# Gate and up projections of two feed-forward blocks by seven block products in place of eight, on one Trainium2 core

## The reference, cut to what matters

```
D_MODEL = 1024
SEQ = 512
D_FF = 2816

def _swiglu(x, w_gate, w_up, w_down):
    return (jax.nn.silu(x @ w_gate) * (x @ w_up)) @ w_down

def first_block(x, ...):
    f = _swiglu(_rmsnorm(x, ffn1_pre_g[l]), ffn1_w_gate[l], ffn1_w_up[l], ffn1_w_down[l])
    x = x + 0.5 * _rmsnorm(f, ffn1_post_g[l])
    ...
    f = _swiglu(_rmsnorm(x, ffn2_pre_g[l]), ffn2_w_gate[l], ffn2_w_up[l], ffn2_w_down[l])
    x = x + 0.5 * _rmsnorm(f, ffn2_post_g[l])
    return x
```

## Time and profile before

| | us |
|---|---|
| median of three runs (2074.23 to 2074.5) | 2074.49 |
| span of the profiled execution, first to last instruction | 2072.8 |
| PE busy in it | 2056.8 (99%) |
| DVE busy | 778.9 (38%) |
| ACT busy | 807.4 (39%) |
| POOL busy | 913.3 (44%) |

### The profile page before, as it was taken

The page is one execution under the profiler, slowest core; times in us unless marked ns, Lnnn a source line. Parts: engine busy times, 40 slices in busy tenths (PEclk is TensorE's granted clock), DMA queues, the critical chain, the costliest instruction groups (busy, mean ns, idle before and its releaser), DMA issues.

```text
span 2072.8 us, 24499 instructions
## 1 busy us (share of the span) xinstructions
PE 2056.8 (99%) x9912; PEld 1694.5 (82%) x9912; DVE 778.9 (38%) x1304; ACT 807.4 (39%) x1421; POOL 913.3 (44%) x468
## 2 busy tenths in 40 slices
PE   9999999999999999999999999999999999999998
PEld 8888888877788888888888887888888788888887
DVE  3111100777844111100356674711132676562112
ACT  4222322467754222222535543522234445352222
POOL 4444444246662444444434442544434443264442
PEclk9999999999999999999999999999999999999999
DMA  6333323221033333222322222333233222223331
GB/s 191 94 101 92 102 92 112 79 72 41 31 102 103 101 93 100 94 99 102 117 91 73 72 82 71 104 100 97 97 111 108 72 74 79 82 92 101 93 102 71
DMA packets 244256, 191.26 MB, mean 92 GB/s; under 512 B 6448, under 2 KB 208816, under 8 KB 243760
## 3 DMA queue, kind: packets, MB, share of 16 engines
q1 hardware_dynamic: 244144, 189.70, 29.7%
HBM read 187.58 MB, written 2.10 MB: 92 GB/s over the span
## 4 chain that ended last, share of the span: by engine, by line
PE 94%; DVE 3%; ACT 1%; issue 1%; SPq 0%; DMA 0%; POOL 0%; DVEq 0%; ACTq 0%
PE bank L1695 29%; PE bank L1697 28%; PE bank L1696 28%; PE bank L1689 3%; PE bank L1929 1%; PE bank L2097 1%; PE bank L1949 1%; PE bank L1956 1%; DVE xn L1158 0%; DVE x_tok L1163 0%; PE bank L2126 0%; PE bank L2128 0%; DVE m_sum L1669 0%; DVE br_lo L1570 0%; DMA w_raw<-in_ffn_w_up 0%
## 5 line engine op out<-in xcount | busy, mean ns | idle before, releaser
L629 POOL TENSOR_TENSOR w_lo<-w_raw,w_hi 128x1024 fp32r<-128x1024 f32 x324 | 783.5, 2428 | 868.6 <-ACT w_hi L723 867.8
L1695 PE MATMUL bank<-xt_hi,w_hi 128*128 128x512 f32 (+1 forms) x1504 | 579.4, 385 | 0.5
L1696 PE MATMUL bank<-xt_lo,w_hi 128*128 128x512 f32 (+1 forms) x1504 | 575.4, 383 | 0.0
L1697 PE MATMUL bank<-xt_hi,w_lo 128*128 128x512 f32 (+1 forms) x1504 | 575.4, 383 | 0.0
L723 ACT ACTIVATE w_hi<-w_raw 128x1024 fp32r<-128x1024 f32 x325 | 340.9, 1053 | 242.9 <-DMA w_raw<-in_ffn_w_down 142.6
L1695 PEld LDWEIGHTS bank<-xt_hi,w_hi 128*128 128x128 f32 x1504 | 282.7, 188 | 62.7 <-issue 6.7
L1697 PEld LDWEIGHTS bank<-xt_hi,w_lo 128*128 128x128 f32 x1504 | 282.7, 188 | 55.6
L1696 PEld LDWEIGHTS bank<-xt_lo,w_hi 128*128 128x128 f32 x1504 | 282.9, 188 | 53.6
L1264 DVE TENSOR_TENSOR h_raw<-bank,act_gate 128x512 f32<-128x512 f32 x44 | 30.4, 691 | 400.1 <-PE bank L1697 400.1
L1695 PE MATMUL bank<-w_hi,xt_hi 128*128 128x512 f32 (+1 forms) x456 | 178.2, 391 | 0.0
L1697 PE MATMUL bank<-w_hi,xt_lo 128*128 128x512 f32 (+1 forms) x456 | 174.5, 383 | 0.0
(11 more groups left out here) (305 smaller groups left out, 2853.9 us busy)
## 6 DMA issues: line engine op xcount, KB each, us to landing
w_raw<-in_w_in SPq DMA_DIRECT2D x132, 512.0 KB, 3.7
w_raw<-in_ffn_w_down SPq DMA_DIRECT2D x44, 512.0 KB, 3.5
w_raw<-in_ffn_w_gate SPq DMA_DIRECT2D x43, 512.0 KB, 3.7
w_raw<-in_ffn_w_up SPq DMA_DIRECT2D x43, 512.0 KB, 3.7
w_raw<-in_w_out SPq DMA_DIRECT2D x24, 512.0 KB, 3.5
w_raw<-in_w_branch SPq DMA_DIRECT2D x24, 512.0 KB, 3.3
w_raw<-in_w_qkv SPq DMA_DIRECT2D x16, 512.0 KB, 3.7
x_tok<-in_x SPq DMA_DIRECT2D x4, 512.0 KB, 6.9
```

Source lines behind the costliest of these rows:

```text
L629: pool.tensor_tensor(lo_slots[i], raw_slots[i], f32(hi_slots[i]), ALU.subtract).then_inc(lo_ready, 1)
L1695: pe.matmul(out_ap, ah, bh, start=first, stop=False)
L1696: pe.matmul(out_ap, ah, bl, start=False, stop=False)
L1697: return pe.matmul(out_ap, al, bh, start=False, stop=last)
```

## The change

From tile 3 on (`F0 = 3`) in both FFNs, the gate and the up slab of a tile are computed together. The weights of a tile form a 2 x 2 matrix of blocks (gate or up; first or second half of the 1024 features), the activation another (half of the features; half of the tokens). Their product takes eight block products, each of 4 x 3 matmuls of 128 x 128 weights on 256 columns. The change uses Strassen's scheme in Winograd's form with seven products and sums of blocks:

- activation sums, once per FFN on DVE (`x_sums`): the four quarters of x as `hi` plus `lo`, then s1 to s4; ACT and DVE split each into `xs_hi`, `xs_lo`;
- weight sums, per tile: t3, t2, t4 by DVE into the banks 6, 7, 4 (`w_sums`), t1 by POOL into `ws_raw1`; ACT makes `ws_hi` of the four, DVE `ws_lo` of three, POOL of t1;
- products, per tile on PE, in this order: first (gate by x) into bank 0 `b_x`; sixth (t2 by s2) into bank 1 `b_y`; the third of the tile before (up by s4) onto bank 2 `b_z`, where the fifth of that tile lies; second (gate by x) onto `b_x`; seventh (t3 by s3) onto `b_y`; fourth (t4 by x) into bank 3 `b_v`; fifth (t1 by s1) into `b_z`;
- between them ACT copies `b_x` (`u1`) before the second product lands on it, DVE forms u2 = `b_y` + u1 before the seventh lands on `b_y`, then u3 = `b_y` + u1, gate of the second token half = u3 - `b_v`, its up = `b_z` + u3 (`up_high`), up of the first half = `b_z` + u2 after the third product, and the two halves of `h_raw`.

`h_raw` now has a place for every tile, with `h_lo` over it, and the split of the hidden features moves from the tile after to the last tile and to the down product. Of an up slab only its second half is split. The core of the diff (names like `b_x`, `nth`, `product_count` are banks and counts of semaphores):

```
+F0 = 3
...
+                for f in range(F0, KF):
+                    if f > F0:
+                        pe.wait_ge(glo_done, nth(n, f - 1))
+                    else:
+                        pe.wait_ge(silu_done, F0 * n + 1)
+                    ready(s0 + 2 * f + 1)
+                    product(b_x, w_quarter(s0 + 2 * f, 0), x_quarter(0, 0)).then_inc(prod_done, 1)
+                    if f > F0:
+                        pe.wait_ge(u3_done, nth(n, f - 1))
+                    else:
+                        pe.wait_ge(silu_done, F0 * n + 2)
+                        pe.wait_ge(xsl_done, 4 * n + 2)
+                    pe.wait_ge(wsl_done, 3 * nth(n, f) - 2)
+                    product(b_y, w_sum(2), x_sum(2)).then_inc(prod_done, 1)
+                    if f > F0:
+                        third_product(f - 1)
+                    pe.wait_ge(u1_done, nth(n, f))
+                    product(b_x, w_quarter(s0 + 2 * f, 1), x_quarter(1, 0), onto=True).then_inc(w_used, 1)
+                    pe.wait_ge(u2_done, nth(n, f))
+                    pe.wait_ge(wsl_done, 3 * nth(n, f) - 1)
...
+                    product(b_y, w_sum(3), x_sum(3), onto=True).then_inc(prod_done, 1)
+                    pe.wait_ge(wsl_done, 3 * nth(n, f))
+                    if f > F0:
+                        pe.wait_ge(hhalf_done, nth(n, f - 1))
...
+                    product(b_v, w_sum(4), x_quarter(1, 1)).then_inc(prod_done, 1)
+                    pe.wait_ge(ws1l_done, nth(n, f))
+                    if f > F0:
+                        pe.wait_ge(h_done, f0 + f)
+                    product(b_z, w_sum(1), x_sum(1)).then_inc(prod_done, 1)
+                third_product(KF - 1)
...
+                x_sums()
+                hidden(0)
+                hidden(1)
+                for f in range(F0 - 1, KF):
+                    last = f == KF - 1
+                    if f == F0 - 1:
+                        x_sum_low(1)
+                        x_sum_low(2)
+                    elif f == F0:
+                        hidden(F0 - 1)
+                    else:
+                        up_high(f - 1)
+                    if not last:
+                        w_sums(f + 1)
+                    if f > F0:
+                        hidden_hi(f - 1)
+                    if f >= F0:
+                        second_sum(f)
+                    if not last:
+                        sum_low(f + 1, 2)
+                    else:
+                        hidden_low(0)
+                        hidden_low(1)
...
+                for f in (2, 3, 4, 5):
+                    hidden_low(f)
+                up_high(KF - 1)
+                hidden_hi(KF - 1)
+                hidden_of_lo(KF - 1)
...
+                    pool.tensor_tensor(ws_raw1[:, :], raw_slots[j][:, 0:512], raw_slots[i][:, 0:512], ALU.subtract)\
+                        .then_inc(ws1_made, 1)
+                    pool.wait_ge(ws1_made, nth(n, f + 1))
+                    pool.wait_ge(ws_made, 3 * nth(n, f + 1))
+                    pool.wait_ge(hi_ready, g + 1)
+                    pool.tensor_tensor(lo_slots[i], raw_slots[i], f32(hi_slots[i]), ALU.subtract).then_inc(lo_ready, 1)
```

More of the change, by code:

```diff
@@ L462, in gate_up_banks, with product_count, nth, wait_raw @@
         def gate_up_banks(f):
-            return ((0, 4), (1, 5))[f] if f < 2 else ((0, 1), (2, 3))[f % 2]
+            return ((0, 4), (1, 5), (2, 3))[f]
+        b_x, b_y, b_z, b_v = (bank[i][:, 0:256] for i in range(4))
+        b_t = {3: bank[6][:, :], 2: bank[7][:, :], 4: bank[4][:, :]}
+        N_F = KF - F0
+        PRODUCTS = {1: 1, 6: 2, 7: 3, 4: 4, 5: 5}
+        def product_count(n, f, i):
+            return 5 * (N_F * n + f - F0) + PRODUCTS[i]
+        def nth(n, f):
+            return N_F * n + f - F0 + 1
+        def wait_raw(eng, s):
+            eng.wait_ge(raw_in[slot_of[s]], 16 * (turn_of[s] + 1))
+        def quads(t):
+            return t.rearrange("p (k n) -> p k n", k=4)
         @block.sync
@@ L684, in _ @@
                     done = slabs_cast(k)
+            lows(done, S_FFN[1] + 2 * F0)
+            ffn(1)
+            done = S_FFN[1] + N_IN
             for l in range(LAYERS):
@@ L805, in hidden_high, with gate @@
                     act.wait_ge(h_done, f0 + 1 + f)
-                    act.activation(h_hi[:, f, :], h_raw[:, f % 2, :], ACT.Copy).then_inc(hhi_done, 1)
-                for f in range(KF):
+                    if f in (0, 6, 12, 14):
+                        act.wait_ge(prod_done, product_count(n, KF - 1, {0: 6, 6: 7, 12: 4, 14: 5}[f]))
+                    if f == 18:
+                        act.wait_ge(w_used, s0 + N_IN)
+                    act.activation(h_hi[f][:, :], h_raw[:, f, :], ACT.Copy).then_inc(hhi_done, 1)
+                def gate(f):
                     act.wait_ge(w_used, s0 + 2 * f + 1)
@@ L1833, in ffn, with x_quarter, x_sum, w_quarter @@
                             turn_chunk(b, 1 + q)
-                for f in range(2, KF):
+                def x_quarter(k0, c0):
+                    sl = slice(256 * c0, 256 * c0 + 256)
+                    return lambda k: (xt_hi[:, 4 * k0 + k, sl], xt_lo[:, 4 * k0 + k, sl])
+                def x_sum(m):
+                    return lambda k: (xs_hi[m][:, k, :], xs_lo[m][:, k, :])
+                def w_quarter(s, k0):
+                    return lambda k: slab(s, 4 * k0 + k, KD, P)
+                def w_sum(m):
+                    return lambda k: (ws_hi[m][:, k, :], ws_lo[m][:, k, :])
@@ new lines, in product, with third_product @@
+                def product(dst, w, x, onto=False):
+                    for k in range(4):
+                        (wh, wl), (xh, xl) = w(k), x(k)
+                        pe.matmul(dst, wh, xh, start=k == 0 and not onto, stop=False, skip_group_check=onto)
+                        pe.matmul(dst, wh, xl, start=False, stop=False, skip_group_check=onto)
+                        ins = pe.matmul(dst, wl, xh, start=False, stop=k == 3, skip_group_check=onto)
+                    return ins
+                def third_product(f):
+                    pe.wait_ge(uphi_done, nth(n, f))
+                    if f == F0:
+                        pe.wait_ge(xsl_done, 4 * n + 4)
+                    ready(s0 + 2 * f + 2)
+                    product(b_z, w_quarter(s0 + 2 * f + 1, 1), x_sum(4), onto=True).then_inc(w_used, 1)
```

247 lines of the change are left out of this document (215 added, 32 removed).

## The result

The changed kernel takes 2060.44 us (median of four, 2059.53 to 2061.28) where the kernel before takes 2074.49: a ratio of 0.9932, 95% interval [0.9918, 0.9946]. It is faster by 14 us, and lies 1.4 above the forecast of 2059. The profiled execution has a span of 2059.5 and a time of 2061.28.

The account below looks back on a forecast made before the run. PE was taken as the bound, busy 99% of the span. The profiled span 2072.8 less 30.4 for the products plus 15.0 for stops gave 2057.4; with 1.7 to the median, 2059 us, range 2047 to 2068.

Parts of the forecast that it names:

- The products: PE's tiles from 3 on: 84 matmuls of 256 columns, 10.08 us instead of 10.88; 30.4 us less over 38 tiles.
- the bound: Border between products on PE: first step 0.20 instead of 0.12, at most 21 us in all; taken as nothing.
- One tile in the middle: Other engines' work lies beside PE; u2, the tightest wait, is there at 3.5 us, wanted at 5.76, 2.2 to spare.
- The unknown price of a sum into a bank: DVE's three sums written into a bank per tile: 0 to 0.69 us more each, u2 still in time; taken as nothing.
- DVE and POOL by turns: At start and end, DVE and POOL on SBUF operands each wait for the other's instruction; even sharing would give 2053.
- The stops: PE waits 2.0 and 1.7 us at each FFN's start, 1.25 and 2.5 at its end; 15.0 in all.
- The clock: Rival: PE's clock falls to 1.2 GHz for a tile behind each of four stops, 31 us more, 2090; chance 0.08.
- A clock below 1.00 behind a stop: Sign in the trace after, named beside a tile of more than 10.3 us, that would make the forecast wrong.
- the stops are hidden: Rival at the FFNs' starts and ends: DVE keeps its turn or queues fall better; 2045.5 to about 2048; chance 0.10.
- DVE's chain replaces PE: Rival in every tile: u2 comes 1.1 us late in 38 tiles, +41, 2100; half of it about 2067; chance 0.11.
- A step for each change of product: Rival on PE: each change of product costs a step, 21 us more, 2080, slower; chance 0.07.

Follow-up runs that it names:

- the last experiment: Changed kernel with six hidden splits behind the last up_hi, DVE making slabs 4 and 5's lo parts, last activation split behind tile 3's u2: 2046.52 us.

## Why the prediction was right, and where it was off

- **The products**, 30.4: right. The tile is 10.08, and the step over a border is 0.12; 0.08 more, the bound, is paid only behind the four stops. The run with the narrow form alone confirms both durations from which the sum was made.
- **One tile in the middle**: right to 0.1. u2 is there at 3.5, with 2.2 to spare; the runs with two and five more sums show that the spare time is real and about that long. The unknown price of a sum into a bank, 0 to 0.69 more, is 0.01.
- **DVE and POOL by turns**: right, and now shown by an experiment and not only by rows. Two turns of POOL in the sums were taken as 4.6; taking POOL's subtractions away gave 38.96 - 34.61 = 4.35. At the end two splits, which alone take 1.25 (four took 2.50), took 4.35 beside POOL and ended 8.8 into the tile (forecast 8.95). The Trainium skill (SBUF — State Buffer, Who interferes with whom) says that issue order decides which of the two blocks; the trace agrees: POOL's own two subtractions took 6.68 and 5.22 there instead of 4.75, and at the end, where POOL began first (235.27), strict turns of 2.4 and 0.6 let POOL end at 240.6 and DVE at 241.2; they ended at 240.49 and 241.04.
- **The stops**: four and no others, each a little shorter than forecast: 1.77, 1.57, 1.13 and 2.27 for 2.0, 1.7, 1.25 and 2.5. The step behind each makes up half of that, so 14.2 stand for 15.0.
- **The clock**: here the forecast was off. Its sum had nothing for the clock, and its rival had it for a whole tile behind each of four stops, 31 us. What came is between: only the stop of 2.1 us lowers it, for 3.4 us, at 1.6 each, up to 3.2 in an execution. The argument against the rival, that no wait had lowered the clock before, rested on waits of at most 1.0 (one of 1.5 stands ahead of PE's first instruction), and the stop priced at 2.5 was beyond them, two and a half times as long and not "up to twice". For that stop the sum had no row at all. A clock below 1.00 behind a stop was also named as a sign that would make the forecast wrong, and it came: the mechanism that it stood for is there, at 1.6 in place of 7.8 per stop, and behind one of the four stops. It cost the median 2.5 (2060.44 against 2057.93 with the stops filled); less the stops' 0.8 and 0.3 of the rest, these are the 1.4 by which the forecast fell short. So the 1.4 is what is left of errors in opposite directions, and the nearness is in part luck.
- **The rivals**: that the stops are hidden is what the last experiment builds (2046.5; the rival said 2045.5 to 2048), so the price was right and the mechanism was not there without the new order. That DVE's chain replaces PE is what the run with five sums builds. A step for each change of product did not come: 0.12 over the border.

## What to carry to other kernels

Price an algorithm with fewer products by the narrower form that it needs: here 12.5% fewer products left 7% of a tile, since a step of 256 columns costs more than half of one of 512. Where the steady tile has slack, look for the loss at its ends, where the added sums meet another engine's work: what the next matmul waits for goes ahead in the queue of the engine that is late, and work wanted later goes behind it. A stop on the engine that bounds costs more than its row says, by what the row leaves out (0.25 us here: 0.16 of the last matmul's way through the array and 0.09 of a slower first step) and, where it was as long as 2.1 us, mostly also by the clock after it.

## What the runs showed of the hardware that was not expected

- The granted clock fell to half for 3.4 us behind 7 of 10 stops of 2.1 us, and behind none of the stops of 1.0 to 1.6 us that were read, among them stops of 1.2 us in one tile after another. Transposes that compute nothing kept it up at no cost.
- Two sums of 1024 elements per partition with both operands in SBUF took 2.36 beside an idle POOL and 4.57 beside a busy one, yet DVE finished POOL's two subtractions in 2.55 where POOL took 6.68 beside it (4.75 alone): handing the work to the faster engine was cheaper than running both.
